# All four gate and up pairs of a feed-forward by seven block products, with a peeled first block

## What is computed

```
D_MODEL = 2048; D_FF = 5632; SEQ = 256

def swiglu(x, w_gate, w_up, w_down):
    return (jax.nn.silu(x @ w_gate) * (x @ w_up)) @ w_down
```

## Time and profile before

| | |
|---|---|
| time of a launch | 2829.12 us, median of 3 (2828.45 to 2832.12) |
| the profiled execution | 2831.91 us, its span 2830.1 us |
| TensorE busy | 2808.7 us, 99% of the span |
| VectorE busy | 2090.1 us, 74% |
| ScalarE busy | 1423.7 us, 50% |
| DMA engines | queue of the loads busy 55.5% of the span |
| granted TensorE clock | 0.998 of full speed on average |

### The profile page before, as it was taken

The page is one execution under the profiler, slowest core; times in us unless marked ns, Lnnn a source line. Parts: engine busy times, 40 slices in busy tenths (PEclk is TensorE's granted clock), DMA queues, the critical chain, the costliest instruction groups (busy, mean ns, idle before and its releaser), DMA issues.

```text
span 2830.1 us, 34324 instructions
## 1 busy us (share of the span) xinstructions
PE 2808.7 (99%) x13238; PEld 2346.9 (83%) x13238; DVE 2090.1 (74%) x2302; ACT 1423.7 (50%) x1626; POOL 14.5 (1%) x20
## 2 busy tenths in 40 slices
PE   9999999999999999999999999999999999999998
PEld 8888888888898788888888888888888888888887
DVE  5469756455565888888888877687788888888885
ACT  5444545454544545445445455755645445444564
POOL 0000000000000000000000000000000000000000
PEclk9999999999999999999999999999999999999999
DMA  7546355555446555555555558543655556565554
GB/s 246 194 161 198 109 184 187 193 178 179 164 150 195 191 188 199 201 200 193 197 198 198 193 158 269 179 156 127 206 189 192 193 192 207 189 207 197 197 190 156
DMA packets 276001, 530.61 MB, mean 187 GB/s; under 512 B 8768, under 2 KB 32464, under 8 KB 275392
## 3 DMA queue, kind: packets, MB, share of 16 engines
q1 hardware_dynamic: 274864, 527.01, 55.5%
q0 software_dynamic: 752, 2.04, 0.2%
q10 hardware_dynamic: 288, 0.20, 0.0%
HBM read 527.12 MB, written 2.10 MB: 187 GB/s over the span
## 4 chain that ended last, share of the span: by engine, by line
PE 91%; DVE 4%; ACT 3%; issue 1%; DMA 1%; SPq 0%; DVEq 0%; ACTq 0%
PE ps L775 20%; PE ps L776 20%; PE ps L778 19%; PE ps L1273 7%; PE ps L1275 7%; PE ps L1274 7%; DVE w_lo L2278 1%; PE ps L784 1%; ACT w_hi L1573 1%; PE ps L803 1%; PE ps L804 1%; PE ps L981 1%; PE ps L808 1%; PE ps L1267 1%; PE ps L961 1%
## 5 line engine op out<-in xcount | busy, mean ns | idle before, releaser
L2278 DVE TENSOR_TENSOR w_lo<-raw,w_hi 128x2048 fp32r<-128x2048 f32 (+4 forms) x358 | 793.9, 2221 | 364.2 <-ACT w_hi L1573 363.3
L775 PE MATMUL ps<-w_hi,x_hi 128*128 128x512 f32 (+4 forms) x2208 | 853.6, 387 | 2.6 <-ACT z L1606 1.0
L1573 ACT ACTIVATE w_hi<-raw 128x2048 fp32r<-128x2048 f32 (+4 forms) x358 | 663.6, 1859 | 377.0 <-DMA raw<-in_ff_w_down 144.0
L776 PE MATMUL ps<-w_lo,x_hi 128*128 128x512 f32 (+4 forms) x2208 | 844.4, 382 | 0.0
L778 PE MATMUL ps<-w_hi,x_lo 128*128 128x512 f32 (+4 forms) x1984 | 757.5, 382 | 0.0
L775 PEld LDWEIGHTS ps<-w_hi,x_hi 128*128 128x128 f32 x2208 | 415.0, 188 | 80.8 <-issue 1.7
L776 PEld LDWEIGHTS ps<-w_lo,x_hi 128*128 128x128 f32 x2208 | 415.2, 188 | 75.8
L778 PEld LDWEIGHTS ps<-w_hi,x_lo 128*128 128x128 f32 x1984 | 372.6, 188 | 70.6
L775 PE MATMUL ps<-w_hi,h_hi 128*128 128x512 f32 x640 | 249.4, 390 | 0.0
L778 PE MATMUL ps<-w_hi,h_lo 128*128 128x512 f32 x640 | 249.2, 389 | 0.0
L776 PE MATMUL ps<-w_lo,h_hi 128*128 128x512 f32 x640 | 249.2, 389 | 0.0
(11 more groups left out here) (423 smaller groups left out, 3306.4 us busy)
## 6 DMA issues: line engine op xcount, KB each, us to landing
raw<-in_w_in SPq DMA_DIRECT2D x139, 1024.0 KB, 5.0
raw<-in_ff_w_gate SPq DMA_DIRECT2D x88, 1024.0 KB, 5.2
raw<-in_ff_w_up SPq DMA_DIRECT2D x88, 1024.0 KB, 5.3
raw<-in_ff_w_down SPq DMA_DIRECT2D x88, 1024.0 KB, 5.1
raw<-in_w_out SPq DMA_DIRECT2D x45, 1024.0 KB, 5.1
raw<-in_w_ple_gate SPq DMA_DIRECT2D x16, 1024.0 KB, 5.1
raw<-in_w_in SPq DMA_DIRECT2D x8, 696.0 KB, 4.2
raw<-in_w_in SPq DMA_DIRECT2D x8, 520.0 KB, 3.7
```

The costliest lines, as they stand in the source:

```text
L775: nc.tensor.matmul(o, x[0][:, k0 + c, s], hi[:, c, 0:width], start=first and c == 0, stop=False)
L776: nc.tensor.matmul(o, x[0][:, k0 + c, s], lo[:, c, 0:width], start=False, stop=False)
L1573: nc.scalar.activation(landed_part(w_hi, u, j), landed_part(raw, u, j), ACT.Copy).then_inc(hi_ready, 1)
L2278: V.tensor_tensor(landed_part(w_lo, u, j), landed_part(raw, u, j), landed_part(w_hi, u, j).bitcast(F32), ALU.subtract).then_inc(parts_read ...
```

## The change

All four pairs are done by sums in the blocks 1 to 9 (`SUMMED`), and the last two pairs alone in block 0 (`SUMMED_FIRST`), which is peeled off the loop; the loop now covers i = 1 to 8. `NS_ALL` counts the pairs by sums of a feed-forward, `sums_before` those ahead of a block. In block 0 the pairs 0 and 1 are plain units, with the transposes between the gate and the up unit of pair 0. The x sums are 512 columns wide and are made between pairs 1 and 2 of block 0, no longer ahead of `first_product`.

In pair 3, now by sums, the plain half of its up product comes last. `shared_done` and the copy of bank 6 wait for pair 3. The first down unit is split ahead of `rests`, the second behind it, on ScalarE likewise (the copy of bank 6 between the two). Down unit 0 of the blocks 0 to 8 uses bank 6 and unit 1 bank 4, as in the loop before; in block 9, unit 0 uses bank 4.

```
--- before.py
+++ after.py
@@ -160,8 +160,9 @@
     TOGETHER = first_unit[MIX_TOGETHER]
     end_unit = [units_of[b][-1] + 1 for b in range(len(blocks))]
 
-    SUMMED = [0, 1, 2]
+    SUMMED, SUMMED_FIRST = [0, 1, 2, 3], [2, 3]
     NS = len(SUMMED)
+    NS_ALL = len(SUMMED_FIRST) + NS * (FB - 2)
 
     HALVED = sorted({first_unit[L1_REST] + 3, first_unit[L1_REST + 4] + 3, first_unit[L1_OUT + 1], first_unit[L1_OUT + 3],
                      first_unit[MIX_OUT + 3]} | set(range(TOGETHER, end_unit[CMP[0]] + 4))
@@ -440,7 +441,15 @@
 
         def down_bank(i, j):
 
-            return 4 + 2 * (j % 2 if isinstance(i, int) else (j + 1) % 2)
+            return 4 + 2 * (j % 2 if isinstance(i, int) and i >= FB - 2 else (j + 1) % 2)
+
+        def summed_of(i):
+
+            return SUMMED_FIRST if isinstance(i, int) and i == 0 else SUMMED
+
+        def sums_before(no, i):
+
+            return no * NS_ALL if isinstance(i, int) and i == 0 else i * NS + (len(SUMMED_FIRST) - NS + no * NS_ALL)
 
         def summed(b):
             return ps[:, 2 * pair_of[b]:2 * pair_of[b] + 2, 0:blocks[b][3]]
@@ -1274,7 +1283,7 @@
                     nc.tensor.matmul(ps[:, bank, :], x[0], w[1], start=False, stop=False)
                     return nc.tensor.matmul(ps[:, bank, :], x[1], w[0], start=False, stop=stop)
 
-                def summed_pair(u, p, n, between=None, before_rest=None):
+                def summed_pair(u, p, n, pairs, between=None, before_rest=None):
 
                     j, k0, q = 2 * p % RAW, p * UC, SUMMED.index(p)
                     gate, up = ([w[:, j + m, :].rearrange("p (k n) -> p k n", k=UC) for w in (w_hi, w_lo)] for m in (0, 1))
@@ -1290,7 +1299,7 @@
                                           bank == 0 and p == 3 and c == 3)
                         return m
 
-                    first, last = q == 0, q == NS - 1
+                    first, last = p == pairs[0], p == pairs[-1]
                     pe.wait_ge(plain_ready, n * 2 + 1)
                     plain(2, gate)
                     if between:
@@ -1298,6 +1307,8 @@
                     if p < 3:
                         pe.wait_ge(plain_ready, n * 2 + 2)
                         plain(0, up)
+                    if first and pairs is SUMMED_FIRST:
+                        pe.wait_ge(xs_ready, (no + 1) * len(xs_runs))
                     pe.wait_ge(ws_ready, n * 2 + 1)
                     three(4, xsum(0), sums(0), first, last)
                     three(5, xsum(1), sums(1), first, last)
@@ -1321,8 +1332,8 @@
                 def down(u, i, last=None):
                     for j in range(4):
                         if j == 0:
-                            pe.wait_ge(rest_summed, i * 2 + (no * 2 * (FB - 1) + 2))
-                        if j == (0 if isinstance(i, int) else 1):
+                            pe.wait_ge(rest_summed, i * 2 + (2 * no * (FB - 1) + 2))
+                        if j == (0 if down_bank(i, 0) == 4 else 1):
                             pe.wait_ge(rest_done, i + (no * (FB - 1) + 1))
                         if j >= 2:
 
@@ -1356,24 +1367,26 @@
 
                 def block_of_hidden(i, last=None):
                     u = i * 12 + (u0 + 8)
-                    n = i * NS + no * NS * (FB - 1)
+                    pairs = summed_of(i)
+                    n = sums_before(no, i)
                     pe.wait_ge(ff_silu, i + (h0 + 1))
                     for p in range(4):
-                        if p == 0:
-                            summed_pair(u, 0, n, lambda: between_halves(i),
-                                        lambda: pe.wait_ge(st_done, i * 2 + (turned_before[hname] + 2)))
-                        elif p in SUMMED:
-                            summed_pair(u + 2 * p, p, n + SUMMED.index(p))
+                        between = (lambda: between_halves(i)) if p == 0 else None
+                        turned = (lambda: pe.wait_ge(st_done, i * 2 + (turned_before[hname] + 2))) if p == pairs[0] else None
+                        if p in pairs:
+                            summed_pair(u + 2 * p, p, n + pairs.index(p), pairs, between, turned)
                         else:
-                            unit(u + 2 * p, 2 * p % RAW, p * UC, UC, BW, 2, False, p == 3)
-                            unit(u + 2 * p + 1, 2 * p % RAW + 1, p * UC, UC, BW, 0, False, p == 3)
+                            unit(u + 2 * p, 2 * p % RAW, p * UC, UC, BW, 2, p == 0, p == 3)
+                            if between:
+                                between()
+                            unit(u + 2 * p + 1, 2 * p % RAW + 1, p * UC, UC, BW, 0, p == 0, p == 3)
                     down(u + 8, i, last)
 
                 all_drained(pe, b)
                 product(u0 + 4, 0)
-                pe.wait_ge(xs_ready, (no + 1) * len(xs_runs))
-                with pe.Fori(0, FB - 2) as i:
-                    block_of_hidden(i)
+                block_of_hidden(0)
+                with pe.Fori(0, FB - 3) as i:
+                    block_of_hidden(i + 1)
                 block_of_hidden(FB - 2, turn_last)
                 down_last(u0 + 12 * FB - 4)
                 at[0] = u0 + 12 * FB
@@ -2071,36 +2084,53 @@
                     nc.scalar.activation(w_hi[:, j + 1, 0:UNIT // 2], raw[:, j + 1, 0:UNIT // 2],
                                          ACT.Copy).then_inc(hi_ready, 1)
 
-                n0 = no * NS * (FB - 1)
                 gate_tanhs(u0, 0)
                 splits(u0 + 6, 2, 2)
-                act.wait_ge(xs_made, 6 * (no + 1))
-                for k, (q0, q1, dst) in enumerate(xs_runs):
-                    nc.scalar.activation(dst[:], xs[:, q0:q1], ACT.Copy).then_inc(xs_hi_ready, 1)
-                pair_hi(u0 + 8, 0, n0)
+                splits(u0 + 8, 0, 2)
+
+                def x_sums_hi():
+                    act.wait_ge(xs_made, 6 * (no + 1))
+                    for k, (q0, q1, dst) in enumerate(xs_runs):
+                        nc.scalar.activation(dst[:], xs[:, q0:q1], ACT.Copy).then_inc(xs_hi_ready, 1)
 
                 def block_of_hidden(i):
                     u = i * 12 + (u0 + 8)
+                    pairs = summed_of(i)
+                    if pairs is SUMMED_FIRST:
+                        splits(u + 2, 2, 1)
                     hidden_hi(i)
                     for p in range(1, 4):
-                        if p in SUMMED:
-                            pair_hi(u + 2 * p, 2 * p % RAW, i * NS + (n0 + SUMMED.index(p)))
+                        if pairs is SUMMED_FIRST and p == pairs[0]:
+                            x_sums_hi()
+                        if p in pairs:
+                            pair_hi(u + 2 * p, 2 * p % RAW, sums_before(no, i) + pairs.index(p))
+                        elif pairs is SUMMED_FIRST and p == 1:
+                            splits(u + 3, 3, 1)
                         else:
                             splits(u + 2 * p, 2 * p % RAW, 2)
-                    act.wait_ge(parts_used, u + (2 * SUMMED[-1] + 1))
+                    if pairs[-1] == 3:
+                        splits(u + 8, 0, 1)
+                    act.wait_ge(parts_used, u + (2 * pairs[-1] + 1))
                     nc.scalar.activation(gate_rest[:, 0], ps[:, 6, :], ACT.Copy).then_inc(p1_copied, 1)
-                    splits(u + 8, 0, 2)
+                    if pairs[-1] == 3:
+                        splits(u + 9, 1, 1)
+                    else:
+                        splits(u + 8, 0, 2)
                     act.wait_ge(gates_summed, i + (no * (FB - 1) + 1))
                     act.wait_ge(hid_ready, i + (h0 + 1))
                     for tt in range(NT):
                         k = nc.scalar.activation(silu[:, tt], gate_rest[:, tt], ACT.Tanh, scale=half_rstd[:, tt:tt + 1])
                     k.then_inc(ff_tanh, 1)
 
-                with act.Fori(0, FB - 2) as i:
+                def whole_block(i):
                     block_of_hidden(i)
                     u = i * 12 + (u0 + 8)
                     splits(u + 10, 2, 2)
-                    pair_hi(u + 12, 0, i * NS + (n0 + NS))
+                    pair_hi(u + 12, 0, sums_before(no, i + 1))
+
+                whole_block(0)
+                with act.Fori(0, FB - 3) as i:
+                    whole_block(i + 1)
                 block_of_hidden(FB - 2)
                 nc.scalar.preload_act_table(ACT.Sqrt)
                 at[0] = u0 + 12 * FB
@@ -3006,10 +3034,10 @@
                     c = i + (no * (FB - 1) + 1)
                     dve.wait_ge(p1_copied, c)
                     V.tensor_tensor(up_rest[:, 0], gate_rest[:, 0], ps[:, 5, :], ALU.add).then_inc(rest_summed, 1)
-                    dve.wait_ge(rest_summed, i * 2 + (no * 2 * (FB - 1) + 1))
+                    dve.wait_ge(rest_summed, i * 2 + (2 * no * (FB - 1) + 1))
                     dve.wait_ge(shared_done, c)
                     V.tensor_tensor(gate_rest[:, 1], up_rest[:, 0], ps[:, 7, :], ALU.add).then_inc(rest_summed, 1)
-                    dve.wait_ge(rest_summed, i * 2 + (no * 2 * (FB - 1) + 2))
```

(41 more changed lines are left out.)

## The result

The changed kernel takes 2838.52 us (median of 7, 2836.08 to 2841.87) against 2829.12 (median of 7, 2828.09 to 2832.12): ratio 1.003, 95% interval 1.002 to 1.004. It is slower by 9.4 us between the medians, 6 to 11 by the interval. The 2838.52 lies in the predicted range (2828 to 2843), 3 us above the predicted 2835.5, on the side (slower) that had the largest chance.

A forecast was written before the change was run, and what follows sets the result against it. TensorE was taken to bound the kernel, busy 99% of the span. 16.6 us less and 22.2 more gave net +5.6: 2837.5 for the profiled execution, 2834.7 at the median, 2835.5 with half the clock term; range 2828 to 2843.

The forecast's parts named there:

- Removed matmuls: Both feed-forwards: 16 more pairs by sums save 3 matmuls each, 48 in all, 10.9 us less.
- The start: Start of each feed-forward: x sums leave it, so both TensorE waits for the first hidden block go, 4.1 us less.
- the sum of 2.9 for each block 0: Peeled first block: later x sums delay sum products by 1.3 us, then last pair and down outputs; 2.9 us more.
- The third down unit: Whole loop blocks: TensorE waits for VectorE's first addition of down outputs, 0.9 us each, 7.2 per feed-forward.
- D: Time mark in each block: start of the first down unit (unit 0); D+11.6 means 11.6 us after it.
- The last block: Each feed-forward's last block: down unit 0 waits for all four additions, 0.9 to 1.0 us; third unit in time.
- The clock term: Behind the first removed wait at the start: lower-clock stretch goes, 1.6 us less in the profiled execution, half for the median.
- That the cover holds: Rival, loop blocks: addition of down outputs ends before the third down unit needs it; 2820 us, chance 0.05.
- that the wait is short: Rival, third down unit: wait of 0.5 us in place of 0.9, near 2828, no change; chance 0.20.
- That VectorE's waits don't shrink: Rival, each round: one more 1 us wait per block stays on TensorE's path, +18, 2853 us; chance 0.10.
- That the clock falls in each wait: Rival: 20 waits of about 1 us each lose 1.6 by lower clock, +32, near 2867 us; chance 0.03.

The follow-up runs named there:

- first experiment: Changed kernel, but in the loop's whole blocks silu and hidden block follow the first addition of down outputs, and ScalarE copies down unit 2 before tanh: 2821.44 us.
- second experiment: Changed kernel, but only the hidden block moved behind the first addition of down outputs, silu and ScalarE's order untouched: 2823.41 us.
- last experiment: Kernel before the change, with silu and hidden block behind the first addition of down outputs and the earlier copy of down unit 2: 2829.13 us.
- fourth experiment: Changed kernel, but the additions of the shared products come ahead of down unit 0's split again, on VectorE and ScalarE: 2856.75 us.
- the one with both repairs: Changed kernel with silu and hidden block behind the first addition of down outputs, and x sums made early behind the first silu: 2815.67 us.

## Why the prediction was right, and where it was off

**Removed matmuls.** 48 fewer, and the round without waits is 63.59 us (first experiment): 0.68 below. As predicted.

**The start.** The two waits for the first hidden block are gone. The wait at block 0's sum products was put at 1.3 and is 1.4, the third down unit's there at 1.2 and is 1.0 by the list and some 0.2 more by the restart. The restart adds 0.2 at the sum products too, and the waits put at 0.3 in the last pair and 0.1 at the first down unit are not in the list. So the sum of 2.9 for each block 0 is met (1.6 and 1.2), but partly because these misses cancel.

**The third down unit.** The path was predicted to end at D+11.6 and ends at D+11.6; the gates start at D+2.89 (2.9), the hidden block at D+6.84 (6.9), the split of unit 2 at D+8.17 (8.2). The price was put at 0.9 a block. By the row above it is 0.94, and against the round of the first experiment (64.45 against 63.59) 0.9. But this wait is shorter than the average of the 16. From the transposes of block 1 to those of block 9, eight rounds, a round takes 64.55 us on average in both feed-forwards; in the kernel before it is 64.25, or 63.57 with 0.68 off for the three matmuls. So the average price is 0.98, and the 16 rounds cost 1.3 us more than was predicted.

**The last block** was mis-sized. Its first down unit was to wait 0.9 to 1.0 with its release, and its third not at all. The list has 1.1 and 0.7 at the first (1.3 and 0.9 with the restart), and 0.2 twice at the third (0.3 each): 2.8 for the two in place of 2.0. The list gives no releaser, but the timeline of the first feed-forward has the cause that was predicted, the last of the four additions:

```profile
1595.58 0.68 DVE L3042 TENSOR_TENSOR z<-z,ps 128x512 f32<-128x512 f32 x1
1596.36 0.47 PE L784 MATMUL ps<-w_hi,h_hi 128*128 128x512 f32 x1 [1.12 <-issue]
```

It ends at 1596.26, 0.10 ahead of the unit. The unit was due at 1595.09, so that is D+1.2 where D+0.7 was predicted: the split of this unit started at D-3.8 in place of D-4.1, and the five operations took 4.9 in place of 4.8.

**The clock term** is the step of the sum that failed. I took the profiled execution (2831.9) as base, let it gain 1.6 for the stretch at the lower clock, and went to the median by taking off 2.8, with half of the 1.6 back. The profiled execution of the changed kernel took 2837.92, the sum said 2837.5. But its median is not 2.8 below it, it is 0.6 above. The 2.8 was not a constant of the profile: over the nine kernels shown here the profiled execution lies between 2.8 above the median (the kernel before) and 1.6 below it (the second experiment). What stands out in the one of the kernel before are two slow stretches, of which the earlier trace rows show one; the second is here, in the kernel before, ahead of the mixer, behind a wait of 1.7 us (the second of the earlier trace rows):

```profile
1641.00:1646.00 5.00, 4.70 (x16) 3.84 (x17) 4.04 (x7) 0.79 (x2) 0.00 (x0) 0.66 0.45 170
```

The last experiment's kernel, whose median differs from that of the kernel before by less than the noise, shows the same two places at full clock (there the wait of 1.7 us ends at 1639.34, and the clock is full from there on too):

```profile
975.50:980.00 4.50, 4.50 (x22) 3.68 (x21) 4.50 (x6) 3.12 (x4) 0.00 (x0) 1.00 0.00 0
1641.00:1646.00 5.00, 5.00 (x27) 4.16 (x26) 4.96 (x7) 2.15 (x5) 0.00 (x0) 1.00 0.02 7
```

In the first it gets through 22 matmuls where the other has 15. Its profiled execution took 2828.6, 3.3 less than 2831.9. Following the same instructions through both traces, each stretch costs 1.6 us, 0.4 of the second is made up again before the next feed-forward, and 0.5 lie ahead of both.

But slow stretches are no property of that one execution. The second place has one in four of the nine kernels' profiled executions: in the kernel before, in the first and the fourth experiment and in the one with both repairs, each time behind the same wait of 1.7 us. In the fourth experiment:

```profile
1652.00:1657.00 5.00, 4.85 (x16) 3.98 (x17) 4.29 (x7) 0.64 (x2) 0.00 (x0) 0.66 0.38 145
```

How many of the executions behind a median have one isn't known, as only the profiled ones have a trace. Without the term, from the median, the sum is 2829.1 - 10.9 - 4.1 + 22.2 = 2836.3; with the last blocks as measured it is 2837.1, and with the average price of the round 2838.4, where 2838.5 was measured. (Agreement to 0.1 is chance: the medians scatter by about 1 us.) The term should have been left out of the median's sum altogether, and the correction with it.

**The rivals.** That the cover holds, and that the wait is short, fell with the rows of the third down unit. That VectorE's waits don't shrink: they did, from 10.7 us a round to 6.4, with none of them on TensorE's path outside the places named. That the clock falls in each wait: 20 waits of up to 1.0 us for `down_added`, and no slow stretch behind them (the mean granted clock is 0.999, 1.00 in both rounds shown above).

## What to carry to other kernels

Before moving work from the engine that is full to one with room, look not at the room in a round but at the moment when each result is due, and at the path that leads there. Here 4.5 us were to fit in 10.7 of idle time and did, while one path ended 0.6 to 1.0 us late in each of 18 blocks. The repair is to look on that path for work that is due much later (the hidden block was made at D+8.2, and its transposes come 108 matmuls and the wait behind D, at D+25.4) and put it behind the result that is due now. And the profiled execution is one execution: compare its own time with the median, and look for what in it is not in the others, before correcting from the one to the other.

## What the runs showed of the hardware

A wait costs TensorE more than the idle time that the profile gives it: 0.68 us of idle at the third down unit was 0.84 of delay at its first matmul and 0.10 more at the second. The 0.16 between the first two is the overlap of matmuls: the next start is due 0.23 behind the last one, and the row gives it a duration of 0.39, from whose end the idle time counts. So a delay of up to 0.16 is in no list of waits; the second experiment has such ones, 0.26 in the round shown with the 0.10 behind it.

Whether the granted clock falls after a wait differs from execution to execution. In the kernel before it fell to its lower level (1.2 GHz) behind one wait of 2.05 us and one of 1.7, and not behind the other, of 2.03. In the last experiment's profiled execution it stayed at the full level behind all three (1.67, 1.71 and 2.00). Behind the wait of 1.7 us ahead of the mixer it fell in four of nine executions. 20 waits of up to 1.0 us in the changed kernel brought no fall, nor did 20 of about 1.6 in the fourth experiment. The Trainium skill, "TensorE: Matmul & The Clock Gate", section "HAM oscillation — how this bites in real kernels", warns of waits that return in each round, with longer waits for a DMA as its example; here, at up to 1.0 us in the changed kernel and 1.6 in the fourth experiment, some 65 us apart, they did no such harm.
